# Order of the long and the short matmuls in the channel mixers, the recurrent mixer and attention of a two-layer trunk

## What is computed

```
h = x
layer 0: h += attention(rmsnorm(h));   h += mlp(rmsnorm(h))
layer 1: h += rglru_block(rmsnorm(h)); h += mlp(rmsnorm(h))
out = rmsnorm(h)

attention:  qkv = hn @ w_qkv + b   (2048 -> 2560: 32 query heads, 4 key and 4 value heads of 64)
            rotary positions, windows of two chunks of 64 tokens, a learned sink per head,
            softmax, then @ w_o + b_o  (2048 -> 2048)
rglru:      proj = hn @ w_in + b   (2048 -> 4096), gelu branch and a causal convolution,
            two gates of 8 blocks 256 x 256, a linear recurrence over tokens,
            (hs * y) @ w_out + b_out   (2048 -> 2048)
mlp:        square(relu(hn @ w_up)) @ w_down   (2048 -> 8192 -> 2048)
```

## Time and profile before

| | |
|---|---|
| median of 3 runs | 1996.04 us (1995.44 to 1996.25) |
| the profiled execution, its own time | 1995.82 us |
| its span, first to last instruction | 1993.7 us |
| TensorE busy | 1982.3 us, 99% of the span |
| TensorE weight loads busy | 1736.9 us, 87% |
| VectorE busy | 1368.5 us, 69% |
| ScalarE busy | 1062.1 us, 53% |
| DMA, share of 16 engines | 55.4%, 184 GB/s read |

### The profile page before, as it was taken

The page is one execution under the profiler, slowest core; times in us unless marked ns, Lnnn a source line. Parts: engine busy times, 40 slices in busy tenths (PEclk is TensorE's granted clock), DMA queues, the critical chain, the costliest instruction groups (busy, mean ns, idle before and its releaser), DMA issues.

```text
span 1993.7 us, 34015 instructions
## 1 busy us (share of the span) xinstructions
PE 1982.3 (99%) x11542; PEld 1736.9 (87%) x11542; DVE 1368.5 (69%) x1575; ACT 1062.1 (53%) x1446; POOL 7.4 (0%) x11
## 2 busy tenths in 40 slices
PE   9999999999999999999999999999999999999998
PEld 8898888888888888888888888888888888888887
DVE  8998676556656665666789997766566556656664
ACT  6666554444444444445588885544444444444453
POOL 1000000000000000000000000000000000000000
PEclk9999999999999999999999999999999999999999
DMA  7434555555555555555555545565556555555652
GB/s 287 158 127 158 181 189 191 188 191 188 189 190 180 197 186 191 177 175 199 190 190 189 189 169 192 188 197 184 193 184 187 192 182 197 189 189 178 195 175 95
DMA packets 104187, 368.17 MB, mean 185 GB/s; under 512 B 11472, under 2 KB 15696, under 8 KB 104016
## 3 DMA queue, kind: packets, MB, share of 16 engines
q1 hardware_dynamic: 103856, 365.53, 55.4%
q0 software_dynamic: 288, 2.10, 0.3%
HBM read 365.48 MB, written 2.10 MB: 184 GB/s over the span
## 4 chain that ended last, share of the span: by engine, by line
PE 94%; DVE 3%; ACT 2%; issue 1%; DVEq 0%; ACTq 0%; POOL 0%; POOLq 0%
PE ps L1307 61%; PE ps L1310 30%; DVE w_lo L812 1%; ACT h L467 1%; PE aux L1327 1%; PE aux L1328 1%; PE aux L1329 1%; PE aux L1399 0%; ACT w_hi L370 0%; DVE h L923 0%; DVE h L934 0%; PE aux L1382 0%; DVE u L826 0%; DVE pt L939 0%; DVE u L899 0%
## 5 line engine op out<-in xcount | busy, mean ns | idle before, releaser
L812 DVE TENSOR_TENSOR w_lo<-w_raw,w_hi 128x1024 fp32r<-128x1024 f32 x678 | 815.8, 1222 | 336.2 <-ACT w_hi L370 335.1
L370 ACT ACTIVATE w_hi<-w_raw 128x1024 fp32r<-128x1024 f32 x678 | 701.4, 1054 | 448.3 <-PE ps L1310 445.5
L1307 PE MATMUL ps<-xn,w_hi 128*128 128x512 f32 x2880 | 906.4, 396 | 0.2 <-DVE w_lo L812 0.2
L1307 PE MATMUL ps<-mid,w_hi 128*128 128x512 f32 x2544 | 799.4, 396 | 1.1 <-DVE w_lo L812 0.6
L1310 PEld LDWEIGHTS ps<-xn,w_lo 128*128 128x128 f32 x2880 | 541.0, 188 | 127.9
L1310 PEld LDWEIGHTS ps<-mid,w_lo 128*128 128x128 f32 x2544 | 477.9, 188 | 113.0
L1310 PE MATMUL ps<-xn,w_lo 128*128 128x256 f32 x2880 | 566.1, 278 | 0.0
L1310 PE MATMUL ps<-mid,w_lo 128*128 128x256 f32 x2544 | 499.9, 278 | 0.0
L1307 PEld LDWEIGHTS ps<-xn,w_hi 128*128 128x128 f32 x2880 | 438.9, 189 | 1.2 <-issue 0.5
L1307 PEld LDWEIGHTS ps<-mid,w_hi 128*128 128x128 f32 x2544 | 387.3, 189 | 1.8 <-DVE w_lo L812 1.0
L826 DVE TENSOR_TENSOR u<-ps,half 128x512 f32<-128x512 f32 x169 | 116.6, 690 | 155.3 <-ACT half L383 136.0
(11 more groups left out here) (168 smaller groups left out, 762.0 us busy)
## 6 DMA issues: line engine op xcount, KB each, us to landing
w_raw<-mlp_w_up_dram SPq DMA_DIRECT2D x256, 512.0 KB, 4.2
w_raw<-mlp_w_down_dram SPq DMA_DIRECT2D x256, 512.0 KB, 4.2
w_raw<-b_w_in_dram SPq DMA_DIRECT2D x64, 512.0 KB, 4.9
w_raw<-a_w_qkv_dram SPq DMA_DIRECT2D x40, 512.0 KB, 4.8
w_raw<-a_w_o_dram SPq DMA_DIRECT2D x32, 512.0 KB, 4.5
w_raw<-b_w_out_dram SPq DMA_DIRECT2D x32, 512.0 KB, 4.4
h<-x_l_dram SPq DMA_DIRECT2D x4, 512.0 KB, 8.1
gate_raw<-b_gate_a_w_dram SPq DMA_DIRECT2D x8, 256.0 KB, 2.8
```

Source lines behind the costliest of these rows:

```text
L370: nc.scalar.activation(w_hi[:, s, :, :], w_raw[:, slot, :, :], ACT.Copy).then_inc(hi_ready, 1)
L812: nc.vector.tensor_tensor(w_lo[:, s, :, :], w_raw[:, slot, :, :], w_hi[:, s, :, :].bitcast(F32), ALU.subtract).then_inc(lo_ready, 1)
L1307: nc.tensor.matmul(ps[:, 2 * half_i + b, :], hi[:, k, b * PART:(b + 1) * PART], operand[:, :, kt, :], start=kt == 0, stop=False)
```

## The change

The chunk's waits, its long matmul and its short matmul become functions of their own, and three orders are made from them:

- `apart`: over the first three chunks (`RUN = 3`) the 24 long matmuls run in a row, then the 24 short ones. The longs of a chunk wait for that chunk as before. `wts_used` of each of the three chunks is raised only by its own last short matmul, behind all 24 longs. The fourth chunk runs in turn.
- in turn: inside a chunk, for b = 0 and then b = 1, over the four k: long, short, long, short. So eight matmuls in a row write to one bank.
- L L S S, as before.

Where they stand: `apart` in the first half of every MLP quad (in the first quad of each MLP in its second half, and its first half stays as it was), in turn in the second half of every other MLP quad (62), in all of quads 1 to 7 of w_in, and in chunks 0 to 2 of six pairs of QKV. The quads of w_o and w_out and the others of QKV and w_in stay. Of 5440 long and as many short matmuls (680 chunks of 8 and 8), 1536 of each are in a run of 24, 3088 of each are in turn, and 816 of each keep their order. No matmul is added or taken away.

```diff
+RUN = 3
-            def products(q, half_i, s, operand, ready_sem, ready, late=False):
+            def chunk_ready(q, half_i, s, ready_sem, ready):
 
                 pe.wait_ge(lo_ready, (q * 2 + half_i) * CHUNKS + s + 1)
                 if s == 0 and not (isinstance(q, int) and q == 0):
                     pe.wait_ge(psum_free, q * 2 + half_i - 1)
                 pe.wait_ge(ready_sem, ready + 2 * s + 2)
+
+            def long(half_i, hi, s, k, b, operand):
+                kt = s * CH_KT + k
+                nc.tensor.matmul(ps[:, 2 * half_i + b, :], hi[:, k, b * PART:(b + 1) * PART],
+                                 operand[:, :, kt, :], start=kt == 0, stop=False)
+
+            def short(half_i, lo, s, k, b, operand):
+                kt = s * CH_KT + k
+                return nc.tensor.matmul(ps[:, 2 * half_i + b, TOK:2 * TOK], lo[:, k, b * PART:(b + 1) * PART],
+                                        operand[:, 0, kt, :], start=False, stop=kt == KT - 1)
+
+            def products(q, half_i, s, operand, ready_sem, ready, late=False, in_turn=False):
+                chunk_ready(q, half_i, s, ready_sem, ready)
                 hi, lo = late_w if late else (w_hi[:, s], w_lo[:, s])
+                if in_turn:
                     for b in range(2):
+                        for k in range(CH_KT):
+                            long(half_i, hi, s, k, b, operand)
+                            last = short(half_i, lo, s, k, b, operand)
+                else:
+                    for k in range(CH_KT):
+                        long(half_i, hi, s, k, 0, operand)
+                        long(half_i, hi, s, k, 1, operand)
+                        short(half_i, lo, s, k, 0, operand)
+                        last = short(half_i, lo, s, k, 1, operand)
                 last.then_inc(wts_used, 1)
 
+            def apart(q, half_i, operand, ready_sem, ready):
+                for s in range(RUN):
+                    chunk_ready(q, half_i, s, ready_sem, ready)
+                    for k in range(CH_KT):
+                        for b in range(2):
+                            long(half_i, w_hi[:, s], s, k, b, operand)
+                for s in range(RUN):
+                    for k in range(CH_KT):
+                        for b in range(2):
+                            last = short(half_i, w_lo[:, s], s, k, b, operand)
+                    last.then_inc(wts_used, 1)
+                for s in range(RUN, CHUNKS):
+                    products(q, half_i, s, operand, ready_sem, ready, in_turn=True)
...
+            def quad_apart(q, operand, ready_sem, ready):
+                apart(q, 0, operand, ready_sem, ready)
+                pair(q, 1, operand, ready_sem, ready, None, whole)
```

More of the change, by code:

```diff
@@ L1303, in products @@
+            def products(q, half_i, s, operand, ready_sem, ready, late=False, in_turn=False):
+                chunk_ready(q, half_i, s, ready_sem, ready)
                 hi, lo = late_w if late else (w_hi[:, s], w_lo[:, s])
-                for k in range(CH_KT):
-                    kt = s * CH_KT + k
+                if in_turn:
                     for b in range(2):
[L1307 to L1311, removed]
@@ L1312, in products @@
-                last.then_inc(wts_used, 1)
-            def pair(q, half_i, operand, ready_sem, ready, between=None):
+                        for k in range(CH_KT):
[7 more added lines that the diff above has]
+                        last = short(half_i, lo, s, k, 1, operand)
@@ L1316, in pair, with quad @@
+            def pair(q, half_i, operand, ready_sem, ready, between=None, in_turn=()):
                 for s in range(CHUNKS):
-                    products(q, half_i, s, operand, ready_sem, ready)
+                    products(q, half_i, s, operand, ready_sem, ready, in_turn=s in in_turn)
                     if between and s in between:
                         between[s]()
-            def quad(q, operand, ready_sem, ready, between=None, between_b=None):
-                pair(q, 0, operand, ready_sem, ready, between)
-                pair(q, 1, operand, ready_sem, ready, between_b)
+            def quad(q, operand, ready_sem, ready, between=None, in_turn=()):
+                pair(q, 0, operand, ready_sem, ready, between, in_turn)
+                pair(q, 1, operand, ready_sem, ready, None, in_turn)
@@ L1414, in attention_pair @@
                     between[2] = lambda: transpose_probs(j - 1)
-                pair(q, half_i, *qkv, between)
+                pair(q, half_i, *qkv, between, (0, 1, 2) if g_before is not None else ())
             attention_pair(1, 1, 0, 0, None)
@@ L1422, in _ @@
                 attention_pair(q, 1, q * 2 - 2, q - 1, q - 2)
+            whole = tuple(range(CHUNKS))
+            def quad_apart(q, operand, ready_sem, ready):
+                apart(q, 0, operand, ready_sem, ready)
+                pair(q, 1, operand, ready_sem, ready, None, whole)
             def late_quad(q, operand, between):
@@ L1446, in mlp @@
                 operand = (xn, xn_ready, 8 * norm)
-                quad(base, *operand, {3: lambda: stats(norm)})
+                pair(base, 0, *operand, {3: lambda: stats(norm)})
+                apart(base, 1, *operand)
                 with pe.Fori(1, 4) as i:
-                    quad(i + base, *operand)
+                    quad_apart(i + base, *operand)
                 with pe.Fori(0, 4) as i:
-                    quad(i + (base + 4), mid, mid_ready, mid_base)
+                    quad_apart(i + (base + 4), mid, mid_ready, mid_base)
                 with pe.Fori(1, GROUPS) as g:
                     with pe.Fori(0, 4) as i:
-                        quad(g * 8 + i + base, *operand)
+                        quad_apart(g * 8 + i + base, *operand)
                     with pe.Fori(0, 4) as i:
-                        quad(g * 8 + i + (base + 4), mid, mid_ready, g * PAIRS + mid_base)
+                        quad_apart(g * 8 + i + (base + 4), mid, mid_ready, g * PAIRS + mid_base)
             mlp(QB_MLP0, 1, MID_MLP0)
@@ L1477, in _ @@
             with pe.Fori(1, GATE_BLOCKS) as n:
-                quad(n + QB_IN, *lru_in, {0: lambda: gates(n - 1)})
+                quad(n + QB_IN, *lru_in, {0: lambda: gates(n - 1)}, whole)
             lru_done = (mid, mid_ready, MID_LRU)
```

## The result

The changed kernel takes 2008.45 us in the median (2008.20 to 2008.66, 4 runs) against 1996.12 us before: a ratio of 1.0062, 95% interval [1.0049, 1.0074]. It is 12.3 us slower. I had forecast 1989 us, and the range ended at 2007. The profiled execution has a span of 2006.2 us against 1993.7.

A forecast was written before the change was run, and what follows sets the result against it. TensorE's pace was taken as the bound: matmul count times spacing, no new waits. 4624 reordered pairs by 1.5 ns gave 6.9 us off 1995.8, so 1988.9, forecast as 1989 us; range 1966 to 2007.

The forecast's parts named there:

- What bounds the kernel: Whole program: TensorE busy 1982.3 of 1993.7 us, so time is number of matmuls times the distance between them.
- Nothing else is late: Whole program: beyond TensorE's waits of 0.8 us for weights and 0.5 us for activations, no waits were seen.
- The waits: MLP halves with `apart`: releases come three in quick order, 2.4 us to spare at the next half; new waits 0.
- The runs: Runs of 24 and 24 in `apart`: 226.7 + 120 = 346.7 ns a pair against 348.2, 1.5 ns less.
- surplus of 13.3: Each matmul, long or short: 13.3 ns beyond its streaming, taken from 256-column runs in attention at 120 ns each.
- The alternating chunks: In-turn chunks, 3088 pairs: uniform order taken to save 1.5 ns a pair; bounds 215 + 113 and 233 + 120.
- The term of -4624 x 1.5 = -6.9 us: All reordered pairs, runs and in turn: each 1.5 ns cheaper, 6.9 us less in all.
- The slower rival: Shorts 120, longs 233: 2003.4 us through `apart`, or 2008 if eight in a row to one bank cost it; chance 0.20.
- its low bound for the in-turn part: Alternating chunks: a pair costs at least 215 + 113 ns, the 113 being the smallest short.

## Why the prediction was wrong

*What bounds the kernel: right.* TensorE's pace is all, and no wait came but 0.3 us. "Nothing else is late" left out 3.3 us of waits in attention and the statistics, which stayed as they were (3.4).

*The waits: right.* The releases came at 6.5 us behind the half's start and three at a time, with the slack that was worked out.

*The runs: steady price right, entry left out.* Shorts at 120.0 and longs at 226.7 once steady, which is the surplus of 13.3 for each that I took from attention. The entry into a run was left out: ten longs at some 6.6 ns more, 4.2 us over 64 halves, less 0.5 us for the first two shorts (113 and 119). So the runs' part of the sum, 1536 x 1.5 = 2.3 us less, came out as 1.1 us more.

*The alternating chunks: the step that failed.* It read: "The 1.5 ns between 346.7 and 348.2 is what I take to come from the meeting of two equal ones after two others, and to go when the order is uniform, in a run or in turn." The steady value is right for one of the two rhythms that alternation has (346.6, in attention and w_in, and in the MLPs of four experiments). I had tacitly given each order one price, and the changed kernel enters the MLPs' alternation in the phase that leads to the other, 353.3. The term of -4624 x 1.5 = -6.9 us came out as +12.6.

*The slower rival* named a time close to the result, 2008, for alternating chunks in the second halves, the right place. That is luck. Its mechanism, eight in a row to one bank, was wrong, and its reading of 120 + 233 as the price was not what the chunks pay (233, 241 and 236 for the longs, 117, 120 and 113 for the shorts). One figure in the forecast is a slip: 0.23 us less 120 ns is 110 ns, not the 113 that its low bound for the in-turn part uses; nothing in the sum rests on it.

*What could have been seen.* The earlier trace rows has both phases: from the longs to the shorts it is 0.47 us (1131.96 to 1132.43) and then 0.46 (1132.66 to 1133.12). I took that for rounding. By the starts in ns it is 470 (an A) and then 463 (a B). A period of eight matmuls in a stream whose pattern repeats after four says that something outlives the pattern, and then a sum over patterns needs the state as well. The trace of before could have raised the chance of "slower"; it has no alternation, so it couldn't have given the 353.

## What to carry to other kernels

Where TensorE is the bound and streams without waiting, the pace of float32r matmuls of mixed lengths can lock into one of several rhythms, 2% apart and for 700 us here (512 and 256 columns, each with its own weights). Before an order is judged by one time, look whether its steps repeat with the pattern or with a multiple of it, and try the same order with one group more or less ahead: 2008.5 and 1989.2 us were the same idea. Two changes that each gain nothing or a little alone can lose together, so time them together.

## What the runs showed that I had not expected

The steady rhythms are near whole multiples of 6.67 ns, which is 16 cycles of 2.4 GHz: a long in a run 226.7 (34), a short 120.0 (18), a cheap pair 346.7 (52), three dear pairs 1060 (159), and two L L S S 1393 (209). The last is odd, so one L L S S is 104 and a half, which would fit that each flips the phase. That starts are tied to such a grid is only inferred from these sums. What in TensorE or its reads keeps the phase, and why each matmul of this kind has 13.3 ns beyond its columns at all, is open; no run here takes it away.
